# Moving the six later modulation parts of each layer: all of them between the merge's projections, none beside the attention branches

## The reference, cut to what matters

```
mod = silu(c) @ w_mod[l] + b_mod[l]                 # (1024) @ (1024, 6*1024), six parts of 1024
h = rms_norm(x, norm_mix_g[l]) * (1 + sc_m) + sh_m
proj = h @ w_in[l]                                   # q, k, v, conv input, ..., and 3*1024 gate columns
y_a = diff_attention(...)  @ w_proj_a                # branch A
y_b = conformer_conv(...)  @ w_proj_b + b_proj_b     # branch B
y_c = stick_breaking(...)  @ w_proj_c                # branch C
merged = g[0] * y_a + g[1] * y_b + g[2] * y_c        # g = sigmoid of the gate columns
x = x + g_m * (merged @ w_out)
... x = x + g_f * moe_ffn(...)
# second block: its own modulation, 2 layers x 3 parts of 1024, for two condition vectors
```

## Time and profile before

| | |
|---|---|
| median of 3 runs | 2931.55 us (2927.52 to 2932.0) |
| the profiled execution | 2933.46 us, its span 2932.2 us |
| TensorE busy | 2731.1 us, 93% of the span |
| VectorE, ScalarE, GpSimd busy | 28%, 20%, 5% |
| weights and other data over DMA | 658.74 MB, mean 225 GB/s |
| branches, layer 0 and layer 1 | 186.8 to 282.3 us, 1162.5 to 1262.3 us |
| merge, layer 0 and layer 1 | 282.3 to 428.2 us, 1262.3 to 1408.2 us |

### The profile page before, as it was taken

One profiled execution on the slowest core, in us unless ns is written; L12 is line 12 of the kernel. 1 busy time (PEld: TensorE's weight loads), 2 busy tenths in 40 slices (PEclk: granted clock), 3 DMA queues, 4 the chain that ended last, 5 costly groups with the idle time before them and its releaser, 6 DMA issues.

```text
span 2932.2 us, 29329 instructions
## 1 busy us (share of the span) xinstructions
PE 2731.1 (93%) x11687; PEld 1654.5 (56%) x11687; DVE 808.2 (28%) x2101; ACT 578.8 (20%) x1163; POOL 160.3 (5%) x191
## 2 busy tenths in 40 slices
PE   6998998999999799899899999978999999897997
PEld 3775994343443376689633433433447766674666
DVE  1374112232222127421222222212322222202242
ACT  2125011010110022420200101102212122203372
POOL 3000000010000000000000000000000000002000
PEclk8999998999999999999899999999999999999998
DMA  9658535999999823464399999994042111003100
GB/s 330 244 202 289 230 133 211 403 416 402 415 415 415 349 87 143 177 230 191 151 380 395 396 417 418 419 395 142 0 138 63 58 58 58 0 0 143 58 1 15
DMA packets 174869, 658.74 MB, mean 225 GB/s; under 512 B 17872, under 2 KB 47848, under 8 KB 122624
## 3 DMA queue, kind: packets, MB, share of 16 engines
q1 hardware_dynamic: 161584, 634.32, 55.3%
q0 software_dynamic: 12704, 22.38, 2.2%
q10 hardware_dynamic: 432, 0.01, 0.0%
HBM read 670.98 MB, written 3.51 MB: 230 GB/s over the span
## 4 chain that ended last, share of the span: by engine, by line
PE 87%; ACT 4%; DMA 4%; DVE 2%; issue 1%; SPq 1%; POOL 1%; DVEq 0%; POOLq 0%; ACTq 0%
PE ps L228 39%; PE ps L1674 15%; PE ps L1724 8%; PE ps L1710 8%; PE ps L1376 2%; PE ps L1655 2%; PE ps L2265 2%; PE ps L500 2%; DMA ring<-in_w 2%; DMA ring<-in_w_mod 1%; PE ps L860 1%; PE ps L1689 1%; PE ps L2718 1%; PE ps L780 1%; PE ps L1642 1%
## 5 line engine op out<-in xcount | busy, mean ns | idle before, releaser
L228 PE MATMUL ps<-hT,ring 128*128 128x256 f32 (+2 forms) x2480 | 667.8, 428 | 4.3 <-ACT xT L1332 3.4
L228 PEld LDWEIGHTS ps<-hT,ring 128*128 128x128 f32 (+1 forms) x2480 | 510.9, 236 | 163.8 <-issue 123.5
L1674 PE MATMUL ps<-ring,ar 128*64 128x512 f32 x2048 | 458.6, 601 | 33.2 <-DMA ring<-in_w 28.8
L1674 PEld LDWEIGHTS ps<-ring,ar 128*64 128x64 f32 x2048 | 151.7, 139 | 329.9 <-issue 326.9
L228 PE MATMUL ps<-ar,ring 128*128 128x256 f32 (+1 forms) x800 | 253.0, 474 | 2.9 <-issue 0.9
L1724 PE MATMUL ps<-ar 128*128 128x512 f32 x528 | 244.2, 605 | 0.0
L1710 PE MATMUL ps<-ring,ar 128*64 128x512 f32 x1024 | 236.2, 604 | 0.0
L228 PEld LDWEIGHTS ps<-ar,ring 128*128 128x128 f32 x800 | 210.1, 324 | 43.2 <-issue 14.7
L1724 PEld LDWEIGHTS ps<-ar 128*128 128x128 f32 x528 | 94.9, 189 | 148.3 <-issue 147.8
L1902 DVE TENSOR_TENSOR ar<-ar,ps 128x256 f32<-128x256 f32 x66 | 27.8, 421 | 474.4 <-ACT ar L1771 474.4
L228 PE MATMUL ps<-ring,hT 128*128 128x256 f32 (+1 forms) x640 | 155.3, 401 | 0.0
(11 more groups left out here) (370 smaller groups left out, 2300.7 us busy)
## 6 DMA issues: line engine op xcount, KB each, us to landing
ring<-in_w SPq DMA_DIRECT2D x384, 1024.0 KB, 11.1
ring<-in_w_mod SPq DMA_DIRECT2D x36, 2048.0 KB, 12.9
ring<-in_w_in SPq DMA_DIRECT2D x16, 2048.0 KB, 14.2
ring<-in_ab_w_in SPq DMA_DIRECT2D x28, 1024.0 KB, 10.0
ring<-in_w_in SPq DMA_DIRECT2D x6, 4096.0 KB, 13.4
ar<-in_w SPq DMA_DIRECT2D x10, 1024.0 KB, 16.0
ring<-in_w_out SPq DMA_DIRECT2D x4, 2048.0 KB, 13.7
ring<-in_ab_w_out SPq DMA_DIRECT2D x2, 4096.0 KB, 12.8
```

The lines of the kernel that those rows point to most:

```text
L228: ins = te.matmul(o, l, r, start=(first and i == 0), stop=(last and i == len(pairs) - 1), skip_group_check=lax)
L1674: ins = te.matmul(b[BOTH[u], :], K.x_b[:, kk, BOTH[u]], w[u][:, :, kk, :], start=(kk == 0), stop=(kk == 7))
```

## The change

The constant `BESIDE` goes. The fifth program of the branches ends with the gate of branch A. Behind the projection of branch A stand later parts 0 to 2, behind that of branch B parts 3 to 5, in TensorE's order, in ScalarE's, in GpSimd's and in the order of the weight loads. VectorE adds up all six behind its last product. No arithmetic is added or removed.

```
@@ ring_plan
         cols(("in", l, 4), I["w_in"][l], 4 * D, D, 4)
-        for key in later_parts(l)[:BESIDE]:
-            mod(*key)
         for b, n in enumerate(("w_proj_a", "w_proj_b", "w_proj_c")):
             if b > 0:
                 cols(("in", l, 4 + b), I["w_in"][l], (4 + b) * D, D, 4)
             rows(("proj", l, b), I[n][l], 4, 2)
-            for key in later_parts(l)[BESIDE + b:BESIDE + b + 1]:
+            for key in later_parts(l)[3 * b:3 * b + 3]:
                 mod(*key)
@@ pe_beside
         yield PAUSE
-    yield from pause(6)
-    yield from pe_mod_later(K, l, 0, BESIDE, 5)
@@ act_beside
         yield PAUSE
-    yield from pause(6)
-    yield from act_mod_later(K, l, 0, BESIDE)
@@ pe_merge
         if br < 2:
-            rows = pe_mod_later(K, l, BESIDE + br, BESIDE + br + 1)
+            rows = pe_mod_later(K, l, 3 * br, 3 * br + 3)
@@ act_merge
-        rows = act_mod_later(K, l, BESIDE + br - 1, BESIDE + br)
+        rows = act_mod_later(K, l, 3 * br - 3, 3 * br)
@@ dve_merge
-    for key in early_parts(l) + later_parts(l)[:BESIDE]:
+    for key in early_parts(l):
         yield from dve_mod_part(K, l, key)
...
-    for key in later_parts(l)[BESIDE:]:
+    for key in later_parts(l):
         yield from dve_mod_part(K, l, key)
@@ pool_branches
-    yield from pool_mods(K, l, 3 if l == 0 else 0, len(early_parts(l)) + BESIDE)
+    if l == 0:
+        yield from pool_mods(K, l, 3, 4)
@@ pool_merge
-    yield from pool_mods(K, l, len(early_parts(l)) + BESIDE, 16)
+    yield from pool_mods(K, l, len(early_parts(l)), 16)
```

More of the change, by code:

```diff
@@ L29 @@
 FIRST = 513 + P
-BESIDE = 4
 BOTH = (slice(0, SLOTS), slice(SLOTS, P))
```

## The result

The median after the change is 3001.7 us (2999.83 to 3003.53, 5 runs) against 2931.55 before (2927.52 to 2935.47 with the runs made beside it): 1.0233 times as long, 95% interval 1.022 to 1.0247. Forecast: 2998.0 us, range 2972 to 3014.

A forecast was written before the change was run, and what follows sets the result against it. The prediction took TensorE, busy 93% of the span, as the bound. 2933.46 us plus 66.4 for weight waits and 0.1 for parts moved gave 3000.0; with the median 1.9 below the profiled execution, 2998 us, range 2972 to 3014.

The forecast's parts named there:

- The weights: Merge, four places: third part's and gate's 8 MB load only after the projection ends; 16.6 us each, 66.4 us in all.
- The parts in the merge: Merge: four more parts of 3.64 us, 14.6 us a layer, all on TensorE's path.
- The branches: Branches: four parts leave, saving 14.5 us a layer, bounds 10.3 to 18.2.
- The third step: Branch C's third step, 29.1 us before, was to take 11 to 19 us; staying above 20 would refute the prediction.
- the halves' share of the chain: Branches' chain of waits: modulation matmuls and ScalarE's row copies take 16.3 us, to be lost less a little.
- Rival 1: Branches: without the halves TensorE may sit at 1.2 GHz, +7 us a layer, 3012 us; chance 0.10.
- Rival 2: Branches don't shrink, as ScalarE's and VectorE's chain sets them and halves only filled gaps; 3027 us; chance 0.06.
- rival 3: Merge: loads behind the projection land as fast as TensorE asks; 2924 us or no change; chance 0.06.
- the expert stages: Expert stages: same order with other ring places, first two experts' weights somewhat earlier, costed at nothing.
- the 3 us that I had named as a sign of being wrong: Expert stages: the prediction is wrong if they change their length by more than 3 us.
- Rival 4: Expert stages: waits for weights near their ends, 13.1 and 15.7 us, both gone: -28.8, 2969 us; chance 0.06.

The follow-up runs named there:

- Experiment 1: Changed kernel, second and third part of each group multiplying with the first part's weights, theirs not loaded: 2927.05 us, 0.9977 of the kernel before.
- 2: Changed kernel, only the third part of each group multiplying with the second part's weights, its own not loaded: 2957.51 us, 1.0088 of the kernel before.
- 3: Kernel before, with two later parts staying in the branches, three behind projection A and one behind projection B: 2972.33 us, 1.0135 of the kernel before.
- 5: Changed kernel, second and third part of each group neither loaded nor computed: 2899.23 us, 0.9882 of the kernel before.
- Experiment 6: Changed kernel plus eight halves' worth of extra matmuls in the branches, without loads, copies or waits: 3003.16 us, 1.0242 of the kernel before.
- 9: Kernel before, with ScalarE's row copies in the branches one round earlier, ahead of a block of silu steps: 2940.06 us, 1.0019 of the kernel before.
- experiment 7: Kernel before, with the router's 1 MB load at ring place 10, which shifts the later places: 2938.38 us, 1.0017 of the kernel before.
- 8: Kernel before, with the router's load at ring place 10 and layer 1's ring places kept as before: 2931.39 us, 0.9986 of the kernel before.

## Why the prediction was right, step by step

**The weights.** Right in mechanism, place and size. Predicted: gate starts 26 us after the projection's end; measured 27.15, 27.28, 26.23 and 25.20. Less the parts' 10.9 us the delays are 16.3, 16.4, 15.3 and 14.3, 62.3 us where 60.4 were forecast; 57.0 of them are idle time, and most of the rest is third parts' halves that ran slower behind their waits, which the prediction counted for the gate alone. The gates are 1.5 to 2.5 us slower, 7.1 where 6.0 were forecast. Together 69.4 against 66.4. Experiment 1 takes the loads away and all of it is gone, 2 takes the third part's away and 44.2 of 74.6 us are gone, 3 shows a site on its own. The estimate came from rows in which three loads restarted the queue; it put the third part at 15.2 us behind the projection's end and the gate's 4 MB 10.4 later, and they came at 16.2 and 10.9 later.

The figure of the Trainium skill ("DMA: Bandwidth & Descriptors", Bandwidth), 425 GB/s for 16 MB, gave an estimate of 8.8 us for each wait, and the trace does not agree for this pattern: 4.2 million bytes in 10.9 us are 385 GB/s, and the first half behind a stopped queue took 8.9 us by itself.

**The parts in the merge.** 3.64 us each was right (3.5 in the difference between experiments 1 and 5).

**The branches.** Predicted saving 14.5 us a layer, bounds 10.3 to 18.2; measured 12.45 and 14.34, of which 1.4 lie in a step without halves. The third step, forecast at 11 to 19 us, took 16.8 and 16.5. The working was less right than the sum: I subtracted the halves' share of the chain as if their matmuls took TensorE's time. Experiment 6 puts the matmuls at 2.65 us in layer 0, two tenths of the saving, and 9 shows that one other place for the copies in ScalarE's order only moved the wait. What the halves cost was mostly that TensorE and ScalarE had to meet eight times in that stretch: 7.2 of layer 0's 9.8 other us are TensorE's waits for the copies. The 2.6 us of slower matmuls that go with them are read from two traces; no kernel had the copies without matmuls. That the sum came so near all the same is in part luck.

**Rival 1, the clock in the branches,** is true in kind and was priced too high, 7 us a layer. The fourth step ran at 0.86 and 0.75 instead of 1.00 and 0.86, and was 1.6 us longer in each layer; with filler it was back at 10.9 us. By the windows of experiment 6 the lower clock costs 5.2 us of busy time in layer 0, of which only part lies on the path. The Trainium skill ("Perfetto Trace Analysis", Matmul Optimizations) says that the matmul engine scales its power with its use, so that matmuls should come back to back in batches. The trace agrees in direction: with 15.0 us of filler in the gaps the granted clock was 1.00 instead of 0.92, and the other matmuls took 5.2 us less.

**Rival 2** (no shrinking) and **rival 3** (weights hidden) are ruled out by the same rows.

**What I costed at nothing: the expert stages.** This is the step that failed. "In the expert stages the order is the same with other places" was true, and the conclusion that it costs nothing was not: the starts of the two expert stages are 3.6 and 3.2 us shorter (the gather's waits alone 7.3 in all), and the experts with their sum 0.9 and 2.7, so that each stage passes the 3 us that I had named as a sign of being wrong. Rival 4 looked for a gain in the wrong wait: the experts' own two waits became 2.9 us shorter, not 28.8. Experiments 7 and 8 show the cause: the ring's places let loads go earlier, so that one stands just ahead of the gather where three stood. The span rose by 68.2 us where 66.5 were forecast, and that they lie so near is in part luck: the stages gave 10.4 us that I had not counted, and against it the merge was 3.1 us worse, the branches saved 2.2 less, the start came 3.2 later, the second block took 2.7 more and layer 1's projections 0.8.

## What to carry to other kernels

When work with streamed weights is moved, lay out the ring by hand and ask for each load which use must end before it may be issued: 8 MB behind one projection was 14 to 14.5 us of idle TensorE, four times, while the queues had stood all but idle for the last 29 us of the branches before it (DMA shares of 0.07 and 0.00 in the windows above). A small edit to the order can put one big load over a recently used place somewhere else in the program, as experiment 7 did, so follow the places to the end. And ask what a piece of work makes two engines do in step, as its own busy time may be the smaller part of its cost.

## What the runs showed of the chip that I had not expected

- Extra matmuls cost little where TensorE is thin. 15.0 us of added matmuls made a stage 2.65 us longer, with the granted clock at 1.00 instead of 0.92.
- The gather of rows suffers from weight loads issued just ahead of it: TensorE waited 9.8 us for the rows with three loads of 1 MB there, and 6.2 with one. The write of the rows ahead of it, 8.7 and 8.4 us, changed little.
- Two loads of 2 MB at the restart of an idle queue, issued 1.9 us apart, landed 9.0 and 16.2 us behind the projection's end, and the 4 MB behind them at 27.1. So the second half came 7.2 us behind the first, though in a full queue two halves land 5.4 us apart. In two other restarts of the same trace, with 0.6 us between the issues (at 231.9 and 348.5 us), it was 6.4 and 5.3; what makes the difference is not shown.
